# Two transformer blocks on one Trainium2 core: layer loops written out, the order of jobs and evictions changed

## The reference, cut to what matters

```
h = rms_norm(x) @ w_in            # latents, differential q/k/v, grouped q/k/v
o_a = attention(6 latent heads);  o_b = differential attention(4 heads);  o_c = grouped attention(6 heads)
x = x + concat(o_a, o_b, o_c) @ w_o
gate, up = split(rms_norm(x) @ w_gate_up)
x = x + (silu(gate) * up) @ w_down
```

```
h = rms_norm(x) @ w_in_2          # pool input a, conv inputs bx bb bc, q, k, v, three gates
br_a = multiscale_pool(a) @ w_branch_a;  br_b = (bb * causal_conv(bc * bx)) @ w_branch_b
br_c = dilated_attention(rope(q), rope(k), v) @ w_branch_c
x = x + rms_norm((g0*br_a + g1*br_b + g2*br_c) @ w_out)
x = x + rms_norm(cross_attention(rms_norm(x), rms_norm(mem)) @ w_mo)
ua, ub = split(rms_norm(x) @ w_up)
x = x + rms_norm((silu(causal_conv(ua)) * ub) @ w_down)
```

## Time and profile before

| | before |
|---|---|
| median of 3 runs | 1926.61 us (1923.85 to 1926.77) |
| the profiled execution's own time | 1928.54 us |
| its span, instructions | 1926.7 us, 35,232 |
| PE, PEld busy | 1782.0 us (92%), 1695.9 us (88%) |
| DVE, ACT, POOL busy | 1210.9 us (63%), 904.3 us (47%), 228.8 us (12%) |
| mean granted TensorE clock | 0.958 of full speed |
| DMA, mean | 144 GB/s |

### The profile page before, as it was taken

How to read it: one execution, slowest core, us unless ns; L and a number is a source line. 1 busy time by engine, 2 the same in 40 slices (tenths; PEclk the granted TensorE clock), 3 DMA queues, 4 the chain that set the end, 5 groups by cost and what they waited for, 6 DMA issues and landing times.

```text
span 1926.7 us, 35232 instructions
## 1 busy us (share of the span) xinstructions
PE 1782.0 (92%) x13736; PEld 1695.9 (88%) x13736; DVE 1210.9 (63%) x1654; ACT 904.3 (47%) x1275; POOL 228.8 (12%) x104
## 2 busy tenths in 40 slices
PE   6998999989998999989999888999799998879997
PEld 6876999989787999989899878999689898879997
DVE  4655577544665766366757757784567657758863
ACT  4454544434555444343443655544434445555542
POOL 3521200015411000010002200000200021010000
PEclk9988999989989999999999998999899999989999
DMA  6320455534212554554434433554344344424551
GB/s 235 118 66 28 158 193 181 185 112 157 94 44 72 197 183 154 181 181 147 138 130 164 153 121 132 166 196 149 135 161 163 105 152 162 153 97 160 195 173 50
DMA packets 52447, 276.60 MB, mean 144 GB/s; under 512 B 5936, under 2 KB 6320, under 8 KB 51888
## 3 DMA queue, kind: packets, MB, share of 16 engines
q1 hardware_dynamic: 51984, 272.14, 41.9%
q10 hardware_dynamic: 288, 2.10, 0.3%
HBM read 273.16 MB, written 1.05 MB: 142 GB/s over the span
## 4 chain that ended last, share of the span: by engine, by line
PE 68%; issue 17%; DVE 9%; ACT 5%; POOL 1%; DVEq 0%; ACTq 0%; POOLq 0%
PE bank L705 17%; PE bank L707 17%; PE bank L708 16%; DVE weights_lo L618 2%; PE scores L1212 2%; ACT weights_hi L607 2%; PE bank L1351 1%; PE bank L1348 1%; PE heads L1227 1%; PE heads L1803 1%; PE bank L714 1%; PE turned L1204 1%; PE bank L716 1%; PE bank L717 1%; PE bank L664 1%
## 5 line engine op out<-in xcount | busy, mean ns | idle before, releaser
L705 PE MATMUL bank<-x_hi,weights_lo 128*128 128x256 f32 (+1 forms) x2512 | 725.4, 289 | 13.4 <-DVE gates L2166 5.1
L707 PE MATMUL bank<-x_lo,weights_hi 128*128 128x256 f32 (+1 forms) x2512 | 715.9, 285 | 0.0
L708 PE MATMUL bank<-x_hi,weights_hi 128*128 128x256 f32 (+1 forms) x2512 | 715.4, 285 | 0.0
L618 DVE TENSOR_TENSOR weights_lo<-raw,weights_hi 128x1536 fp32r<-128x1536 f32 (+2 forms) x302 | 522.0, 1749 | 259.1 <-ACT weights_hi L607 258.6
L607 ACT ACTIVATE weights_hi<-raw 128x1536 fp32r<-128x1536 f32 (+3 forms) x352 | 501.0, 1442 | 259.3 <-PE bank L708 178.1
L705 PEld LDWEIGHTS bank<-x_hi,weights_lo 128*128 128x128 f32 (+1 forms) x2512 | 485.0, 193 | 23.4 <-issue 5.9
L707 PEld LDWEIGHTS bank<-x_lo,weights_hi 128*128 128x128 f32 (+1 forms) x2512 | 485.4, 193 | 2.1 <-issue 2.0
L708 PEld LDWEIGHTS bank<-x_hi,weights_hi 128*128 128x128 f32 (+1 forms) x2512 | 485.2, 193 | 0.0
L631 POOL TENSOR_TENSOR weights_lo<-raw,weights_hi 128x1536 fp32r<-128x1536 f32 (+4 forms) x50 | 165.3, 3316 | 1053.6 <-ACT weights_hi L607 1053.5
L705 PE MATMUL bank<-hidden_hi,weights_lo 128*128 128x256 f32 x704 | 198.0, 281 | 6.6 <-DVE weights_lo L618 5.1
L707 PE MATMUL bank<-hidden_lo,weights_hi 128*128 128x256 f32 x704 | 197.4, 280 | 0.0
(11 more groups left out here) (315 smaller groups left out, 2616.0 us busy)
## 6 DMA issues: line engine op xcount, KB each, us to landing
raw<-in_w_b SPq DMA_DIRECT2D x194, 768.0 KB, 4.7
raw<-in_w_a SPq DMA_DIRECT2D x122, 768.0 KB, 4.4
raw<-in_w_a SPq DMA_DIRECT2D x14, 512.0 KB, 3.6
raw<-in_w_b SPq DMA_DIRECT2D x10, 512.0 KB, 4.1
mem<-in_mem ACTq DMA_DIRECT2D x2, 1024.0 KB, 4.9
raw<-in_w_a SPq DMA_DIRECT2D x2, 752.0 KB, 4.1
raw<-in_w_b SPq DMA_DIRECT2D x2, 752.0 KB, 4.5
raw<-in_w_b SPq DMA_DIRECT2D x2, 720.0 KB, 5.1
```

The source lines that it names most:

```text
L618: nc.vector.tensor_tensor(wlo[c % SPLIT][:, 0:n], raw[c % RAW][:, 0:n], whi[c % SPLIT][:, 0:n].bitcast(F32), ALU.subtract).then_inc(*s.mar ...
L705: ins = nc.tensor.matmul(dst, wl, xh, start=start, stop=False, skip_group_check=skip)
L707: nc.tensor.matmul(dst, wh, xl, start=False, stop=False, skip_group_check=skip)
L708: ins = nc.tensor.matmul(dst, wh, xh, start=False, stop=stop, skip_group_check=skip)
```

## The change

It does the following.

1. The loops over the layers are written out on all engines and SP; wait values are constants, and gains are read from the table of both layers without a copy.
2. At "down3" ACT and POOL split chunks 0 and 1 of the next layer. "first_chunks" (new, at the head of both lists) does the same for the first.
3. The additions of squares ("adds") stand one job ahead of "mean", and POOL's part with them.
4. The feed-forward's evictions are four entries of their own (ffn_in, ffn_hi or ffn_taps, ffn_lo, ffn_out), each a job later than before, and three more banks (`ring`) serve gate, up, o3, ua and ub. "ahead" splits one chunk more before the last hidden_lo.
5. First block: gv goes to slot 2, uv0 and uv1 to slots 5 and 6, dif_sum ahead of uv0, dif_spread behind the scores of slot 7; part0 to part2 one slot earlier (with 6, 7 and 8 slices of mix); o3 comes first of the output jobs, its head in slot 12.
6. Second block: a0, a1 and the conv jobs come after q1, then k1, q2, k2, v0, v1; "prepare" stands ahead of q2. POOL takes the chunks of a0 to k1.

```diff
-    for i in range(3):
-        job(f"part{i}", "w_o", "mix", cols(i * T, 2), mix[:7], part="first")
+    early = (6, 7, 8)
+    for i in range(3):
+        job(f"part{i}", "w_o", "mix", cols(i * T, 2), mix[:early[i]], part="first")
+    job("o3", "w_o", "mix", cols(3 * T, 2), mix)
...
+        ring = bank + score_bank + [out_bank]
...
+        def scalar_next_chunks(pl, act, l):
+            after, m = next_layer(pl, l)
+            if after:
+                here, layer = pl.hi_next, pl.s.layer
+                after.hi_next, after.s.layer, after.s.writing = 0, m, "scalar"
+                split_hi(after, act, m, 1)
+                pl.hi_next, pl.s.layer = here, layer
+                after.hi_ahead = 2
...
         def start_use(pl, pe, l, name):
-            n = pl.uses[name]
-            if n >= BANKS:
-                pe.wait_ge(*pl.s.at(l, *pl.freed[n - BANKS]))
-            return bank[n % BANKS]
+            n = pl.at[name]
+            if n in ring_free:
+                pe.wait_ge(*ring_free[n])
+            ring_free[n] = pl.s.at(l, *pl.freed[name])
+            return ring[n]
...
-        order_a += [("job", "cq0"), ("job", "cq1"), ("mean", "n1"), ("job", "ckv"), ("factor", "n1"), ("job", "kr"), ("job", "dq0")]
+        order_a += [("job", "cq0"), ("job", "cq1"), ("adds", "n1"), ("job", "ckv"), ("mean", "n1"), ("job", "dq0"), ("factor", "n1"), ("job", "kr")]
...
-        after = {0: [("job", "dv0"), ("spread_keys", "dk1")], 1: [("job", "dv1"), ("keys", 0)], 2: [("job", "uk0"), ("job", "uk1")],
+        inside.update({6: [("spread_keys", "uk0"), ("spread_keys", "uk1"), ("spread_keys", "uk2")], 7: [("dif_spread", 0)], 12: [("root_table", "o"), ("job", "o3")]})
+        after = {0: [("job", "dv0"), ("spread_keys", "dk1")], 1: [("job", "dv1"), ("keys", 0)], 2: [("job", "uk0"), ("job", "uk1"), ("job", "gv")],
                  3: [("job", "uk2"), ("job", "uq0")], 4: [("job", "uq1"), ("job", "uq2")],
-                 5: [("job", "gv"), ("job", "uv0"), ("job", "uv1"), ("dif_sum", 0), ("roots", "mla")],
-                 6: [("spread_keys", "uk0"), ("spread_keys", "uk1"), ("spread_keys", "uk2"), ("dif_spread", 0)], 7: [("dif_out", 0)],
-                 9: [("job", "part0")], 10: [("job", "part1")], 11: [("job", "part2")]}
+                 5: [("dif_sum", 0), ("roots", "mla"), ("job", "uv0")], 6: [("job", "uv1")], 7: [("dif_out", 0)],
+                 8: [("job", "part0")], 9: [("job", "part1")], 10: [("job", "part2")]}
...
+        order_b += [("job", "q0"), ("adds", "n1"), ("job", "k0"), ("mean", "n1"), ("job", "q1"), ("factor", "n1"), ("turn", "q0"), ("job", "a0"), ("turn", "k0"),
+                    ("job", "a1"), ("turn", "q1"), ("job", "bx01"), ("job", "bxb2"), ("job", "bb01"), ("job", "bc01"), ("job", "bc2"),
+                    ("job", "k1"), ("job", "q2"), ("turn", "k1"), ("job", "k2"), ("turn", "q2"), ("job", "v0"), ("turn", "k2"), ("job", "v1")]
+        order_b.insert(order_b.index(("job", "q2")), ("prepare", 0))
...
-        plan_b.of_pool = {0, 1}
+        plan_b.of_pool = {0, 1} | plan_b.chunk_range("a0", "k1")
...
-            with pe.Fori(0, DEPTH) as l:
+            for l in range(DEPTH):
```

More of the change, by code:

```diff
@@ L354, in mark @@
         keys = self.marks.setdefault(what, [])
-        assert key not in keys, (what, key)
-        keys.append(key)
+        assert (key not in keys) == (self.layer == 0), (what, key)
+        if self.layer == 0:
+            keys.append(key)
         self.last[self.writing] = what, key
@@ L362, in own @@
         return self.at(layer, *self.last[self.writing])
-    def previous(self, layer, what):
-        return self.sem(what), layer * len(self.known.get(what, "?")) + self.start(what)
     def start(self, what):
@@ L1099, in transformer @@
[L1099 to L1102 removed]
+        order_a += [("job", "o0"), ("front", ("n2", 3)), ("job", "o1"), ("front", ("n2", 0)), ("job", "o2"), ("front", ("n2", 1)),
+                    ("front", ("n2", 2)), ("job", "gate0"), ("adds", "n2"), ("job", "up0"), ("mean", "n2"), ("job", "gate1"), ("factor", "n2"),
+                    ("ffn_in", 0), ("job", "up1"), ("ffn_out", 0)]
@@ L1104, in free_a @@
+        for i in range(2, KF // 2):
+            order_a += [("job", f"gate{i}"), ("ffn_hi", i - 2), ("ffn_in", i - 1), ("job", f"up{i}"), ("ffn_lo", i - 2), ("ffn_out", i - 1)]
+        n = KF // 2 - 1
+        order_a += [("ffn_hi", n - 1), ("ffn_in", n), ("ffn_lo", n - 1), ("ffn_out", n), ("ffn_hi", n), ("ahead", f"up{n}"), ("ffn_lo", n)]
+        order_a += [("job", "down0"), ("root_table", "down")] + [("job", f"down{i}") for i in range(1, 4)]
         def free_a(name):
@@ L1301, in tensor_a @@
         def tensor_a(pe, l):
+            A.layer = l
             A.writing = "tensor"
@@ L2365, in pool_layer @@
                     pool_lo(pl, pool, l, pl.last_chunk(name) + 2)
+                    if name == "down3":
+                        pool_next_chunks(pl, pool, l)
         @block.gpsimd
         def _(pool):
-            with pool.Fori(0, DEPTH) as l:
+            for l in range(DEPTH):
                 pool_layer(plan_a, pool, l, order_a)
-            with pool.Fori(0, DEPTH) as l:
+            for l in range(DEPTH):
                 pool_layer(plan_b, pool, l, order_b)
@@ L2382, in _ @@
                 dve.wait_ge(loaded[n], 16)
-            with dve.Fori(0, DEPTH) as l:
+            for l in range(DEPTH):
                 vector_a(dve, l)
@@ L2396, in _ @@
                 act.wait_ge(loaded[n], 16)
-            with act.Fori(0, DEPTH) as l:
+            for l in range(DEPTH):
                 scalar_a(act, l)
@@ L2402, in _ @@
             load_root_table("second")
-            with act.Fori(0, DEPTH) as l:
+            act.wait_ge(loaded["gains_b"], 16)
+            for l in range(DEPTH):
                 scalar_b(act, l)
```

239 lines of the change are left out of this document (136 added, 103 removed).

## The result

| | before | changed |
|---|---|---|
| median | 1925.69 us (4 runs) | 1956.33 us (1951.42 to 1961.99, 4 runs) |
| ratio | | 1.0161, 95% interval 1.0130 to 1.0192 |
| profiled execution's own time, its span | 1928.5, 1926.7 us | 1951.42, 1949.6 us |
| PE busy, PE idle in the span | 1782.0, 144.7 us | 1773.0, 176.6 us |

The changed kernel is slower by 1.6%. The forecast of 1868 us and its range are missed, and so is its sign. PE's busy time fell by 9.0 us (the matmuls are the same, so this is the clock); its idle time rose by 31.9 us where the forecast had it fall by 36.7 (54.7 less the 18 of the new stall).

What follows compares the result with a forecast made beforehand. PE bounds the kernel, busy 1782.0 of 1926.7 us. Waits of 54.7 us plus 25.4 of clock, less 22 for a new stall, give 58.1 us won: 1868 us against the median, own range 1852 to 1884, wider range 1838 to 1896.

Steps and rivals of the forecast that it cites:

- layer starts: PE's gaps at the kernel's start and three later layers shrink through loop, copy and early chunks: 21.6 us won.
- sums of a norm: PE's waits before the sums of squares: additions a job ahead remove all six, 13.9 us.
- feed-forward: DVE's chunks and hidden_lo: Second block's down0: two waits for DVE's chunks, 2.6 us each, go through the chunk split ahead; 5.1 us won.
- attention: First block's slots: 13.6 us of transpose waits go, new waits at dif_sum and gate0 cost 4.6; net 9.0 us.
- gates: PE's two waits for DVE's eviction of the gates go, as conv and "prepare" lie before k2: 5.1 us.
- before bb01: Second block: POOL's chunks hold DVE's windows ahead of turn q1; PE waits 9 us a layer, 2 more for clock.
- clock (busy time): PE regains clock where waits go: 25.4 us, between 0 and 38.5; about 2 us a layer lost behind the stall.
- The step that failed: Inside the feed-forward: later evictions hold banks longer, but six banks suffice; nothing either way.
- Rival A: Second block: DVE is not held by POOL, no stall before bb01; 1846 us, chance 0.25.
- Rival C: Layer boundaries: chunks 0 and 1 not ready, POOL or the slot late, boundaries stay; 1893 us, chance 0.05.
- Rival B: PE's waits close but its clock doesn't return, since small matmuls and not gaps lower it; 1893 us, chance 0.2.
- Rival D: Whole kernel slower: written-out program is one straight instruction stream, each engine waits for it; 1952 us, chance 0.05.

Runs made afterwards that it cites:

- e2: Changed kernel with ACT's and DVE's feed-forward orders of the second block as before, six-bank ring and PE's order kept: 1895.6 us, ratio 0.982 to the kernel before.
- e1: Changed kernel with DVE's eviction entries put ahead of the job's chunk in the second block's feed-forward (from ua2 on): 1898.2 us.
- e8: Kernel before with DVE's chunk put ahead of its share of the eviction in the second block's feed-forward: 1977.4 us, ratio 1.029.
- e3: Changed kernel with the second block's chunks a0 to k1 given back from POOL to DVE: 1930.2 us.
- e5: Changed kernel without the early splitting of the next layer's chunks 0 and 1 beside down3: 1959.8 us.
- e9: Kernel before with its nine hardware layer loops written out, nothing else changed: 1921.6 us, ratio 0.999.
- b1: Changed kernel with DVE's evictions ahead of its chunks, POOL out of a0 to k1 and the last branch chunk, POOL splitting o3's chunks: 1847.1 us.
- b3: b1 with DVE also making mc3's eviction and the reciprocal of the memory's norm ahead of a chunk: 1852.9 us, ratio 0.964 to the kernel before.
- e7: Changed kernel with the first block's attention slots put back as in the kernel before, o3 staying in slot 12: 1966.9 us.
- e4: Changed kernel with DVE's pool windows moved behind turn q1, POOL keeping its chunks: 1943.1 us.
- e6: Changed kernel with POOL also splitting the chunks of o3 in the first block: 1950.9 us.

## Why the prediction was wrong, point by point

The ledger of PE's idle time, in us, forecast against measured (from the waits of the two kernels):

| term | forecast | measured |
|---|---|---|
| layer starts | -21.6 | 40.3 to 20.3: -20.0 |
| sums of a norm | -13.9 | 13.9 to 6.4: -7.5 |
| feed-forward: DVE's chunks and hidden_lo | -5.1 | 9.0 to 53.1: +44.1 |
| attention | -9.0 | transposes -12.3, dif_sum +3.9, gate0 +1.0, heads +7.6: +0.2 |
| gates | -5.1 | -5.1 |
| before bb01 | +18 | +19.2 |
| x_lo, norm factors, squares around p1 | 0 | +3.5 + 5.1 + 0.3 = +8.9 |
| others (mk0's chunk, merge_part, root) | 0 | -8 |
| sum | -36.7 | +31.9 (rows add to +31.8) |
| clock (busy time) | -25.4 + 4 | -9.0 |

**The step that failed** is "the later evictions inside the feed-forward hold banks longer, but the ring has six, and PE never waited there: nothing either way". I costed the lag and the banks, rightly as e2 shows, and didn't see that the same edit moved DVE's share of the eviction from ahead of its chunk to behind it. PE never waited there because of that place. It could have been read beforehand: the earlier trace rows has no wait there, but a chain of 0.68 + 0.91 + 1.47 + 1.76 + 1.78 + 0.63 + 2.07 + 0.63 + 1.47 + 1.76 = 13.2 us against 11.4 us of matmuls stands in the durations, and the order of DVE's instructions shows it closed. e1 (-58 us) and e8 (+53 us in the other kernel) settle this cause from both sides. With it mended (e1) the kernel takes 1898 us, still 30 above the 1868 forecast: idle is 124.1 us where the forecast had 108.0, and busy is 1772.6 where it had 1760.6. So beside the failed step some 16 us of waits and 12 of clock were mis-sized, by the ledger's other rows. The forecast's own range was also too narrow for its parts: a stall of 4 to 15 us a layer and half of the clock up or down give 1845 to 1893 us when both fall the same way, not 1852 to 1884.

**The stall before bb01** was forecast with place, cause and size: 9 us a layer, 9.6 measured; DVE's windows "over 3 us each", 3.37 and 4.27 measured. Rival A (DVE is not held, 0.25) did not come. What the prediction left at nothing is that the same chunks also hold the additions of n1 (see e3). The section of the Trainium skill that I cited ("SBUF — State Buffer", "SBUF: two separate sides") has the operation that starts first keep the ports for its length. The trace agrees as far as POOL's operations go; of DVE's queued windows keeping the ports, as I read it for rival A, it shows the opposite: POOL got in behind each one that it held, three chunks in 12.17 us.

**Layer starts**: right in size (20.0 for 21.6), half wrong in cause. I named loop, copy and early chunks; the early chunks are worth 2.5 us of the waits (e5) and the loops 4.8 (e9). The remaining 13 lie in the copy and in the place of ACT's first chunks, which I didn't name, and the runs don't part these two. Rival C (chunks 0 and 1 not ready) did not come. At the kernel's start, where I expected 0.3 us less, the changed kernel's profile has 1.1 more; the variants, with the same start, have 14.7 to 16.0, so this is the first transfer's own spread.

**Norm sums**: four of six, not six. The four of n2 and n3 went; the first block's n1 kept 1.1 and 1.4 us, and the second block's n1 got two new ones of 2.0 and 1.9, which e3 shows to be POOL's chunks again.

**Attention**: the transposes went as forecast (17.1 to 4.8 us, under 6 as I named). dif_sum cost 3.9 where I took 2.3, gate0 1.0 where I took 2.3. Not seen was o3 inside slot 12: its chunk fell to DVE, ahead of mix_lo, 4.6 us a layer. The prediction has no term for o3 at all, neither for its matmuls nor for its chunk.

**Around p1** 8.9 us: a chunk on DVE ahead of the last branch evictions and of the memory's reciprocal, where before none or one stood. e3 and b1 keep these waits, so it isn't POOL; b3, with DVE's order changed, takes them back to the values of before.

**The clock** was to give 25.4 us, less 4 behind the new stalls; it gave 9.0. In the first block busy time fell from 769.1 to 753.0 us, in the second it rose from 1013.0 to 1020.0: new waits cost there what the old ones gave back. Rival B (small matmuls, not gaps, lower it) is refuted where it was argued: the same stretch has 1.00 with the 48 short matmuls of gv in slot 2 and 0.57 without. The feed-forward with its start and end has 0.94 now, and 0.99 in b1 (1110 to 1300). b1, with the waits gone, is 1782.0 - 1754.7 = 27 us better in busy time than the kernel before. Of the Trainium skill's two causes ("TensorE: Matmul & The Clock Gate", "HAM oscillation — how this bites in real kernels" for long gaps, "A second HAM failure mode: psum-queue depth-cycling" for micro-idles between groups) the trace agrees in attention with the gap: the 0.57 of e7 stands around one wait of 3.3 us. The 1.3 us before the first norm's sum are no long gap, and the clock fell behind them in the kernel before (0.72), while in the changed kernel, behind a wait of 1.1 us at the same sum, it stayed at 1.00 (33 to 43 us); what lowered it there no run shows.

**Rival D** (slower, by instruction supply) had the right sign and the wrong mechanism: e9, written out like the change, is no slower than the loops (0.997 to 1.000), and PE's waits for issue in the changed kernel sum to 0.3 us.

## What to carry to other kernels

When an edit moves an engine's shares of a job, write down for each pair of engines that hand things to each other which one is ahead of the other, and add up the chain of one period if neither is; a chain longer than the matmuls it feeds is paid in every period, though each of the two engines has idle time. Look for the sign in the waits of the engine that makes weights: as long as it waits for TensorE, it is ahead. Give an engine's urgent small work (evictions, low parts) its place ahead of its long work (chunks), and after each edit that shifts chunk borders or owners check what stands behind a chunk.

## What the runs showed of the hardware that was not expected

- A held operation pays by its place and not by its size: 96 x 16 elements took 3.37 us beside POOL's chunks and 0.17 alone, 20 times as long; an operation with one SBUF tensor and a constant in the same place took 0.27 and 0.28. In e4 POOL was idle from 848.6 to 850.3, and the 96 x 768 addition and the small product that began there took 0.94 and 0.17 us; the next two, with POOL back at work, 3.37 and 3.73.
- The clock makes a kernel's time spread. The four runs of e2 took 1906.1 and 1902.6 us at a mean granted clock of 0.964 and 0.961, and 1888.7 and 1884.1 at 0.972 and 0.975. The kernel before, with its waits in fixed places, ran from 1917.9 to 1929.7 us, the runs of one variant lie up to 1.2% apart; PE's busy time differs by 10 us between two kernels whose waits differ in little more than one kind (e6 and the changed one). By these spreads I estimate that a difference of medians below some 5 us shows nothing here; the waits in the trace do.
- Waits taken away one by one gave 90 us, together 109. The idle time fell by about the same both ways (84.0 and 85.1 us), and the rest is busy time: 1754.7 us in b1 against 1772.6 to 1782.8 in e1, e3 and e6.
